# The second block's sequence and context as two instruction streams in turn

## The chip, the core and the metric

The kernel runs on one core of a Trainium2 chip. The number that counts is the time of one execution on the device, in microseconds (us); the runs give a median and a spread, and one further execution was recorded by the hardware profiler. Five engines take part: TensorE (PE, matmuls, with its weight loads PEld), VectorE (DVE), ScalarE (ACT), GpSimd (POOL) and SyncE (SP), which issues the loads. Each engine works through a queue of its own in order and waits for the others by semaphores.

## What is computed

Two transformer blocks in a row, all in float32. The first has one stream of 512 tokens. The second has two: the sequence (512 tokens, `h`) and a context (256 tokens, `hc`), which share all weights. Of the reference, the second block is what matters here:

```python
for i in range(DEPTH_2):                      # 2 layers
    last = i == DEPTH_2 - 1
    h = ffn_half_step(h, g_ffn1[i], m[0], m[1], m[2], w13_ffn1[i], w2_ffn1[i])
    hc = ffn_half_step(hc, g_ffn1[i], mc[0], mc[1], mc[2], w13_ffn1[i], w2_ffn1[i])
    z = n_lat @ w_in[i]
    zc = n_ctx @ (w_in[i][:, OFF_KV:OFF_G] if last else w_in[i])
    # keys and values of both; the sequence attends to both, the context to itself
    y = mix_heads(z, jnp.concatenate([k, kc], axis=1), jnp.concatenate([v, vc], axis=1), rope, *mix_p) @ w_out[i]
    h = h + m[5] * y
    h = ffn_half_step(h, g_ffn2[i], m[6], m[7], m[8], w13_ffn2[i], w2_ffn2[i])
    if not last:
        yc = mix_heads(zc, kc, vc, None, *mix_p) @ w_out[i]
        hc = hc + mc[5] * yc
        hc = ffn_half_step(hc, g_ffn2[i], mc[6], mc[7], mc[8], w13_ffn2[i], w2_ffn2[i])
```

A half step is a norm, `silu(a) * b` of two products 1024 by 2816, and a product back to 1024. `mix_heads` joins a Fourier mixer, attention, a gated mixer and a pooling mixer. So the sequence's attention of a layer needs the context's keys and values of that layer, and those need the context's first half step of that layer; nothing of the context needs the sequence.

## The kernel before

Tokens lie on the free axis and features on the partitions, so a product is 128 output features at a time: 8 tiles of 128 input features, each in three matmuls (`products`, L1753 to L1755), since a float32 operand is split in a high and a low part. A weight block of 128 columns is thus 24 matmuls of 512 columns for the sequence and 24 of 256 for the context.

A block goes through four stages: SP loads it into one of 4 `stage` buffers (`load_block`), ACT copies the high part into one of 3 slots (`split_block`, L1455), DVE (even block numbers, L2129) or POOL (odd ones, L1381) subtracts it for the low part, and PE uses it. `weights` asks for the next split block when it hands out the current one, and that is where the next block's copy stands in ACT's queue.

The code is a walk in Python that every engine makes for itself; each keeps the calls that are its own. The order of the walk is the order of every queue. Small closures are let in at fixed places: `jobs`, and `background`, one piece of the modulation each (a load of 512 KB, 2 + 14 operations of DVE, L2181 and L2184, one small matmul L1775), of which `have_vectors` forces those that are needed.

In the second block `half_step` takes both streams: `swiglu` fetches a block once and multiplies sequence and context with it, in groups of 8, 8 and 6 tiles of the hidden features (`GROUPS`); after a group the products back (`w_down`) are summed into `h`. A background job stands at each tile and at each of the 8 output tiles of a group. Then `mixers` runs for the context and then for the sequence, each alone; in layer 1 the context's stops at keys and values. Before each part stands a norm: squares, a sum by a matmul of ones (L1767), root and reciprocal (`residual_root`), and 8 tiles of `norm_tile` and `norm_low`. The banks 0 to 3 of PSUM are `banks` (products), 4 to 7 `mix` (all else); attention takes all eight in pairs.

## Time and profile before

| | us |
|---|---|
| median of 3 runs | 4099.03 |
| lowest, highest | 4095.73, 4102.06 |
| the profiled execution | 4101.93 |
| its span, first to last instruction | 4100.1 |
| PE busy | 3692.7 (90%) |
| DVE busy | 2276.9 (56%) |
| ACT busy | 1086.1 (26%) |
| POOL busy | 803.9 (20%) |

Of the span, the first block takes the first 1114 us, the rest is the second block. PE is busy in nine tenths of it; the mean clock that it was granted is 0.941 of full speed. In the 40 slices of the page PE's digit falls to 5 to 8 in four places of the second block, where the feed-forward parts end and the norms and mixers stand, and the clock's digit falls with it.

### The profile page before, as it was taken

The numbers are of one execution on the slowest core, as the hardware profiler recorded it, in microseconds if no ns is written. First come the engines' busy times: TensorE is split into PE (matmuls) and PEld (weight loads), VectorE is DVE, ScalarE is ACT, GpSimd is POOL, SyncE is SP. The second block draws the span as 40 slices with busy tenths as digits, with TensorE's granted clock in tenths as the row PEclk, the third lists the DMA queues.
The fourth block names the chain that finished last, engine by engine and source line by source line (L and its number), as shares of the span: only waits on it lengthen the run. The fifth ranks groups of instructions, "written<-read, shape, count | busy, mean of one in ns | idle before, by whom it ended". The sixth has DMA issues, their size and how long they took to land. (4 is left out here: it accounts for less than half of the span.)

```text
span 4100.1 us, 47478 instructions
## 1 busy us (share of the span) xinstructions
PE 3692.7 (90%) x19008; PEld 2977.6 (73%) x19008; DVE 2276.9 (56%) x4939; ACT 1086.1 (26%) x1685; POOL 803.9 (20%) x488
## 2 busy tenths in 40 slices
PE   5888997999889999877889999998999997888997
PEld 3655885788678888755447888887888884457886
DVE  5564556755566666744445666686666534434333
ACT  3354002322321211233243212123212133333222
POOL 1012101222330101223113121232000032012222
PEclk9998787999999999988999999998999997999999
DMA  5532003444323333333102333332333312112332
GB/s 158 149 98 69 1 1 88 113 118 123 88 65 98 105 99 103 94 90 98 42 16 81 85 108 98 108 98 77 93 108 99 92 48 81 32 41 82 93 93 67
DMA packets 663805, 348.35 MB, mean 85 GB/s; under 512 B 29989, under 2 KB 658919, under 8 KB 663328
## 3 DMA queue, kind: packets, MB, share of 16 engines
q1 hardware_dynamic: 662432, 342.69, 29.8%
q8 instruction: 149, 2.44, 0.3%
q10 hardware_dynamic: 1152, 2.62, 0.2%
q14 instruction: 72, 0.59, 0.0%
HBM read 340.55 MB, written 4.72 MB: 84 GB/s over the span
## 5 line engine op out<-in xcount | busy, mean ns | idle before, releaser
L1753 PE MATMUL psum<-hn_high,high 128*128 128x512 f32 (+2 forms) x3360 | 1234.2, 367 | 133.1 <-DVE hn_low L2159 58.4
L1755 PE MATMUL psum<-hn_high,low 128*128 128x512 f32 (+2 forms) x3360 | 1207.2, 359 | 0.0
L1754 PE MATMUL psum<-hn_low,high 128*128 128x512 f32 (+2 forms) x3360 | 1204.1, 358 | 0.0
L1381 POOL TENSOR_TENSOR low<-stage,high 128x1024 fp32r<-128x1024 f32 (+2 forms) x195 | 478.0, 2460 | 2253.3 <-ACT high L1455 2253.3
L1753 PEld LDWEIGHTS psum<-hn_high,high 128*128 128x128 f32 (+1 forms) x3360 | 641.6, 191 | 264.4 <-DVE hn_low L2159 62.7
L2184 DVE SCALAR_TENSOR_TENSOR partial<-stage,cond,partial 128x128 f32<-128x128 f32 x2304 | 819.8, 429 | 0.0
L1755 PEld LDWEIGHTS psum<-hn_high,low 128*128 128x128 f32 (+1 forms) x3360 | 640.3, 191 | 103.7 <-issue 1.8
L1754 PEld LDWEIGHTS psum<-hn_low,high 128*128 128x128 f32 (+1 forms) x3360 | 642.2, 191 | 95.9 <-issue 2.1
L1455 ACT ACTIVATE high<-stage 128x1024 fp32r<-128x1024 f32 (+3 forms) x440 | 438.1, 1016 | 523.3 <-DMA stage<-in_w_ffn 353.8
L1753 PE MATMUL psum<-hidden_high,high 128*128 128x512 f32 (+1 forms) x1408 | 503.8, 358 | 8.8 <-POOL low L1381 8.7
L1755 PE MATMUL psum<-hidden_high,low 128*128 128x512 f32 (+1 forms) x1408 | 496.6, 353 | 0.0
L1754 PE MATMUL psum<-hidden_low,high 128*128 128x512 f32 (+1 forms) x1408 | 494.9, 352 | 0.0
L2129 DVE TENSOR_TENSOR low<-stage,high 128x1024 fp32r<-128x1024 f32 (+2 forms) x245 | 335.2, 1379 | 173.8 <-ACT high L1455 173.6
L2416 DVE TENSOR_TENSOR tmp<-tmp,psum 128x512 f32<-128x512 f32 (+1 forms) x176 | 103.3, 587 | 392.1 <-PE psum L1755 392.0
L1459 ACT ACTIVATE hidden_high<-tmp 128x512 fp32r<-128x512 f32 (+1 forms) x176 | 97.2, 552 | 812.8 <-DVE tmp L2416 812.8
L1753 PEld LDWEIGHTS psum<-hidden_high,high 128*128 128x128 f32 x1408 | 268.2, 190 | 46.8 <-POOL low L1381 11.8
L1754 PEld LDWEIGHTS psum<-hidden_low,high 128*128 128x128 f32 x1408 | 268.1, 190 | 37.2
L1755 PEld LDWEIGHTS psum<-hidden_high,low 128*128 128x128 f32 x1408 | 267.2, 190 | 37.7
L1646 ACT ACTIVATE tmp<-psum 128x512 f32<-128x512 f32 (+1 forms) x176 | 91.3, 519 | 383.2 <-PE psum L1755 383.1
L2134 DVE TENSOR_TENSOR hidden_low<-tmp,hidden_high 128x512 fp32r<-128x512 f32 (+1 forms) x176 | 104.3, 593 | 108.9 <-ACT hidden_high L1459 108.9
L2413 DVE TENSOR_TENSOR tmp<-tmp,psum 128x512 f32<-128x512 f32 (+1 forms) x176 | 102.3, 581 | 102.8 <-ACT tmp L1646 102.7
L1775 PEld LDWEIGHTS psum<-ones,partial 128*128 128x128 f32 x768 | 112.6, 204 | 54.0 <-DVE partial L2184 41.6
(308 smaller groups left out, 3342.7 us busy)
## 6 DMA issues: line engine op xcount, KB each, us to landing
stage<-in_w_ffn SPq DMA_DIRECT2D x240, 512.0 KB, 4.5
stage<-in_w_ada SPq DMA_DIRECT2D x192, 512.0 KB, 4.0
stage<-in_w_in SPq DMA_DIRECT2D x56, 512.0 KB, 5.1
stage<-in_w_out SPq DMA_DIRECT2D x32, 512.0 KB, 4.1
stage<-in_w_ffn SPq DMA_DIRECT2D x32, 384.0 KB, 4.4
stage<-in_w_gate SPq DMA_DIRECT2D x22, 512.0 KB, 4.0
stage<-in_w_up SPq DMA_DIRECT2D x22, 512.0 KB, 5.2
stage<-in_w_down SPq DMA_DIRECT2D x16, 512.0 KB, 4.5
```

Of the source, the lines that this page charges most:

```text
L1381: self.e.tensor_tensor(low, raw, high.bitcast(F32), ALU.subtract).then_inc(*self.mark("split", n))
L1455: self.e.activation(high, raw, ACT.Copy).then_inc(*self.mark("high", n))
L1459: self.e.activation(high, x, ACT.Copy).then_inc(*self.mark("high_half", key))
L1753: self.e.matmul(out, high[:, i], xh, start=first and i == 0, stop=False)
L1754: self.e.matmul(out, high[:, i], xl, start=False, stop=False)
L1755: done = self.e.matmul(out, low[:, i], xh, start=False, stop=last and i == nk - 1)
L1775: done = self.e.matmul(bank.ap[:, at:at + 1], part.ap[:, i, :], self.mem.ones[:, 0:1], start=both or i == 0, stop=both or i == 1)
L2129: self.e.tensor_tensor(low, raw, high.bitcast(F32), ALU.subtract).then_inc(*self.mark("split", n))
L2134: self.e.tensor_tensor(low, x, high.bitcast(F32), ALU.subtract).then_inc(*self.mark(*key))
L2184: self.e.scalar_tensor_tensor(acc, view[:, k, :], by, acc, ALU.mult, ALU.add).then_inc(*inc)
L2413: self.e.tensor_tensor(s, s, ps_a, ALU.mult).then_inc(*self.mark("gated", key))
L2416: self.e.tensor_tensor(s, s, ps_b, ALU.mult).then_inc(*self.mark("gated_up", key))
```

## The change

The second block becomes two generators. `lead_stream` is the sequence, `side_stream` the context. Each step of them ends in a `yield` with a number, the time for which the stream is taken to have nothing to do, on a clock that `cost` advances by the estimated time of PE. `together` takes the steps in turn: the sequence's whenever it is due, the context's when it is not (the other way round while the context is `urgent`, in its layer 0 mixers). The result is one fixed order for each engine.

- `swiglu` and `half_step` take one stream. The context's half steps (three of them) fetch and split all weight blocks for themselves, in groups of 4, 4, 4, 4, 3 and 3 tiles (`GROUPS_SIDE`); their blocks back are 4 tiles by 256 columns (`wide`). The sequence's first half step of layer 0 has groups of 6, 6, 5 and 5 (`GROUPS_BESIDE`), the others keep 8, 8 and 6.
- A background job stands at each tile of the sequence, at every second output tile of it, and at every second tile of the context.
- Memory: one map for the second block (`block_maps`). The context has temporaries of its own (`side_tmp`), sequence and context have two product banks each, the sequence's attention two pairs and two single banks.
- The table of the token Fourier transform and the gated mixer's weights come through the stages.
- In the mixers the sections `v` and `u` alternate by tile, and steps are split where the other stream may come in. The sequence waits for the context's keys and values before its attention, and in layer 0 for all of its mixers.

The counts of matmuls are the same, 9792 of 512 columns and 5280 of 256 in the products. Of the splits of weight blocks of 384 to 1024 columns there are 670 where there were 434: ACT copies 552 blocks of 1024 columns for 388, DVE subtracts 291 for 220, POOL 261 for 168, and small blocks of 384 to 768 columns come to 118 for 46. ACT_TABLE_LOAD stands 52 times for 32.

```diff
+GROUPS_BESIDE = ((0, 6), (6, 6), (12, 5), (17, 5))
+GROUPS_SIDE = ((0, 4), (4, 4), (8, 4), (12, 4), (16, 3), (19, 3))
...
+    def together(self, lead, side):
+
+        ready = {lead: self.now, side: self.now}
+        while ready:
+            streams = [x for x in ((side, lead) if self.side.urgent else (lead, side)) if x in ready]
+            due = [x for x in streams if ready[x] <= self.now]
+            stream = due[0] if due else min(streams, key=ready.get)
+            self.now = max(self.now, ready[stream])
+            gap = next(stream, None)
+            if gap is None:
+                del ready[stream]
+            else:
+                ready[stream] = self.now + gap
...
     def modulated_norm(self, name, part, gain, shift, after):
+
         T = part.T
         self.bring_two()
-        rinv, ready, t = self.residual_root(part, name)
+        yield from self.residual_root(part, name)
+        rinv, ready, t = self.rooted
...
+        yield 4.0 + T / 128
...
+            if k < KT + 1:
+                yield T / 450
...
-    def swiglu(self, name, parts, w_a, a0, w_b, b0, w_down, gate, meanwhile=None):
...
-                order = list(enumerate(parts))
-                for n, part in order if at else order[::-1]:
...
+    def swiglu(self, name, part, groups, hidden, w_a, a0, w_b, b0, w_down, gate, meanwhile=None):
+
+        T = part.T
+        halves = ((0, KT // 2), (KT // 2, KT)) if part is self.main else ((0, KT),)
+        for first, tiles in groups:
+            wide = tiles == 4
             for f in range(tiles):
                 at = first + f
...
+                yield 0
+                n, slot, view = self.weights(w_b, 0, KT, b0 + at * P)
+                if at and (part is self.main or at % 2):
                     self.pump_background()
...
+                self.gate_tile(key, bank_a.ap[:, 0:T], t, s)
+                bank_a.free = [("gated", key)]
+                bank_b = part.banks.next()
...
+                self.up_tile(key, bank_b.ap[:, 0:T], s, hidden[0][:, f, :], hidden[1][:, f, :], part.hidden_free)
+                bank_b.free, t.free = [("gated_up", key)], [("hidden", key)]
+                yield 0
...
+                if self.events and part is self.main and f % 2:
                     self.pump_background()
...
     def second_block(self):
-        main, side = self.main, self.side
-        for layer in range(2):
...
-            self.half_step([main, side], layer, "g_ffn1", 0)
-            self.mixers(side, layer, layer == 1)
-            self.mixers(main, layer, False)
...
+        mem, main, side = self.mem, self.main, self.side
+        main.banks, side.banks = Turn(self.banks.spots[0:2]), Turn(self.banks.spots[2:4])
+        self.events.add("second")
+        self.together(self.lead_stream(), self.side_stream())
+        self.whole(self.plain_norm(main, "final2", False))
...
+    def lead_stream(self):
+
+        main, hidden = self.main, self.mem.hidden
+        yield from self.plain_norm(main, "final", True)
+        for layer in range(2):
+            yield from self.half_step(main, layer, "g_ffn1", 0, *((GROUPS, hidden["whole"]) if layer else
+                                                                  (GROUPS_BESIDE, hidden["beside"])))
+            while layer == 0 and "side mixed" not in self.events:
+                yield 3.0
+            yield from self.mixers(main, layer, False)
+            self.boundary(("mixed", layer))
+            main.hidden_free = [("all", ("mixed", layer), x) for x in COMPUTE]
+            yield from self.half_step(main, layer, "g_ffn2", 6, GROUPS, hidden["whole"])
+
+    def side_stream(self):
+
+        side, hidden = self.side, self.mem.hidden["side"]
+        yield from self.half_step(side, 0, "g_ffn1", 0, GROUPS_SIDE, hidden, normed=True)
+        side.urgent = True
+        yield from self.mixers(side, 0, False)
+        side.urgent = False
+        self.events |= {"side mixed", ("kv", 0)}
+        self.boundary("side mixed")
+        side.hidden_free = [("all", "side mixed", x) for x in COMPUTE]
+        yield from self.half_step(side, 0, "g_ffn2", 6, GROUPS_SIDE, hidden)
+        yield from self.half_step(side, 1, "g_ffn1", 0, GROUPS_SIDE, hidden)
+        while ("attention", (0, "main")) not in self.events:
+            yield 3.0
+        yield from self.mixers(side, 1, True)
+        self.events.add(("kv", 1))
```

PE's new order in the second block, in words: 648 of the context's matmuls within the two norms in front of the sequence's first half step; that half step of the sequence (22 tiles) with two blocks of the context in it; then the rest of the context's first half step (888 matmuls of 256 columns) and all its mixers with nothing beside them; then the sequence's mixers with the context's second half step let in, 24 matmuls at a time, up to the sequence's next norm and the one before layer 1; then the sequence's mixers of layer 1 with the context's third half step let in; 1200 matmuls of that half step and the context's keys and values with nothing beside them; then the sequence's attention and what follows, alone.

Three places show it. First ACT in the feed-forward parts of layer 1. Before, both streams' tiles stand between two pairs of copies:

```order
L1455 ACTIVATE high_5_53<-stage_51 128x1024
L1455 ACTIVATE high_6_54<-stage_51 128x1024
L1646 ACTIVATE tmp_58<-psum 128x512
L1459 ACTIVATE hidden_high_126<-tmp_58 128x512
L1646 ACTIVATE tmp_58<-psum 128x256
L1459 ACTIVATE hidden_high_122<-tmp_58 128x256
```

And now ACT where the context runs alone, the same place in layer 1:

```order
L1615 ACTIVATE high_6_54<-stage_51 128x1024
L1615 ACTIVATE high_4_52<-stage_51 128x1024
L1806 ACTIVATE side_tmp_126<-psum 128x256
L1619 ACTIVATE hidden_high_124<-side_tmp_126 128x256
L1615 ACTIVATE high_5_53<-stage_51 128x1024
```

A pair of copies now stands at every tile of 256 columns; the first of a pair (the block of the `up` product of the same tile) stands behind the tile before's `hidden_high`.

Second ACT in the attention of the sequence in layer 0. Before, exponentials and turned weights alone:

```order
L1721 ACTIVATE scores_175,small_67<-psum,small_67 128x768
L1728 ACTIVATE weights_t_174<-psum 128x6x128
L1721 ACTIVATE scores_175,small_67<-psum,small_67 128x768
L1728 ACTIVATE weights_t_174<-psum 128x6x128
L1721 ACTIVATE scores_175,small_67<-psum,small_67 128x768
```

Now:

```order
L1883 ACTIVATE scores_177,small_67<-psum,small_67 128x768
L1615 ACTIVATE high_5_53<-stage_51 128x1024
L1806 ACT_TABLE_LOAD
L1806 ACTIVATE side_tmp_126<-psum 128x256
L1619 ACTIVATE hidden_high_124<-side_tmp_126 128x256
L1890 ACTIVATE weights_t_175<-psum 128x3x128 x2
L1883 ACT_TABLE_LOAD
L1883 ACTIVATE scores_176,small_67<-psum,small_67 128x768
```

The context's copies, its sigmoid and its `hidden_high` came between the rows, with two table loads around them.

Third DVE at the products back of a half step in layer 0. Before, one job stands at each output tile:

```order
L2181 TENSOR_SCALAR partial_68<-stage_51,cond_65 128x128 x2
L2184 SCALAR_TENSOR_TENSOR partial_68<-stage_51,cond_65,partial_68 128x128 x14
L2189 TENSOR_SCALAR mod_0_15_63<-psum,vec_61 128x2
L2294 SCALAR_TENSOR_TENSOR h_main_49<-psum,small_67,h_main_49 128x512
```

Now, in the group of 5 tiles, one at every second:

```order
L2458 SCALAR_TENSOR_TENSOR h_main_49<-psum,small_67,h_main_49 128x512 x2
L2345 TENSOR_SCALAR partial_68<-stage_51,cond_65 128x128 x2
L2348 SCALAR_TENSOR_TENSOR partial_68<-stage_51,cond_65,partial_68 128x128 x14
L2353 TENSOR_SCALAR mod_0_15_63<-psum,vec_61 128x2
L2293 TENSOR_TENSOR low_8_56<-stage_51,high_5_53 128x640
```

The job moved from every output tile of both streams to every second one of the sequence.

## Rows read from the trace of the kernel before

**Rows 1.** Windows: from:to, length; busy us (instructions) of each engine; clock, DMA share, GB/s.
```profile
1114.00:1148.00 34.00, 10.68 (x55) 7.45 (x53) 23.83 (x19) 9.54 (x15) 15.08 (x10) 0.65 0.11 31
...
1733.00:1855.00 122.00, 82.46 (x460) 65.71 (x460) 56.27 (x119) 47.54 (x103) 28.07 (x27) 0.82 0.29 79
1855.00:1894.00 39.00, 25.33 (x194) 23.94 (x194) 15.20 (x20) 14.30 (x21) 16.26 (x13) 0.89 0.38 113
1894.00:2051.00 157.00, 127.96 (x470) 77.86 (x470) 65.61 (x96) 44.59 (x68) 33.84 (x26) 0.86 0.22 63
2051.00:2125.00 74.00, 60.37 (x208) 29.57 (x208) 34.48 (x72) 32.36 (x55) 0.00 (x0) 0.91 0.00 0
2125.00:2179.00 54.00, 46.87 (x192) 36.98 (x192) 18.96 (x27) 20.86 (x32) 24.20 (x19) 0.97 0.27 79
2179.00:2221.00 42.00, 35.10 (x169) 28.33 (x170) 27.79 (x41) 15.89 (x23) 17.84 (x12) 0.92 0.17 48
...
2778.00:2836.00 58.00, 42.48 (x183) 34.11 (x184) 34.84 (x66) 25.16 (x41) 20.84 (x19) 0.76 0.23 64
...
3366.00:3408.00 42.00, 22.97 (x96) 16.27 (x94) 18.93 (x30) 17.08 (x34) 10.43 (x13) 0.71 0.20 63
3408.00:3567.00 159.00, 128.59 (x470) 78.26 (x470) 66.04 (x97) 44.58 (x68) 33.79 (x26) 0.86 0.21 60
3567.00:3641.00 74.00, 60.38 (x208) 29.59 (x208) 34.43 (x72) 32.82 (x56) 0.00 (x0) 0.91 0.00 1
```

**Rows 2.** PE's matmuls in order of time: start, length (they overlap), line, operands.
```profile
1108.15 0.39 PE L1753 MATMUL psum<-hidden_high,high 128*128 128x512 f32 x1
1108.38 0.39 PE L1754 MATMUL psum<-hidden_low,high 128*128 128x512 f32 x1
...
1141.79 0.28 PE L1753 MATMUL psum<-hn_high,high 128*128 128x256 f32 x1
1141.91 0.28 PE L1754 MATMUL psum<-hn_low,high 128*128 128x256 f32 x1
```

**Rows 3.** The context's w_out alone, 1870 to 1882, in order of time, four engines.
```profile
1870.07 0.48 DVE L2294 SCALAR_TENSOR_TENSOR h_ctx<-psum,mod,h_ctx 128x256 f32<-128x256 f32 x1 [1.11 <-PE psum L1755]
...
1870.59 0.42 ACT L1477 ACTIVATE tmp<-h_ctx 128x256 f32<-128x256 f32 x1 [2.89 <-DVE h_ctx L2294]
1870.91 1.05 ACT L1455 ACTIVATE high<-stage 128x1024 fp32r<-128x1024 f32 x1
...
1872.04 2.36 POOL L1381 TENSOR_TENSOR low<-stage,high 128x1024 fp32r<-128x1024 f32 x1 [0.21 <-ACT high L1455]
...
1874.45 0.38 PE L1753 MATMUL psum<-mixed_high,high 128*128 128x256 f32 x1 [1.70 <-POOL low L1381]
...
1881.87 0.38 PE L1753 MATMUL psum<-mixed_high,high 128*128 128x256 f32 x1 [1.70 <-POOL low L1381]
```

**Rows 4.** DVE's job beside and without POOL's subtractions, feed-forward part of layer 0.
```profile
1415.20 3.75 DVE L2184 SCALAR_TENSOR_TENSOR partial<-stage,cond,partial 128x128 f32<-128x128 f32 x14
...
1429.42 8.07 DVE L2184 SCALAR_TENSOR_TENSOR partial<-stage,cond,partial 128x128 f32<-128x128 f32 x14
...
1429.67 5.04 POOL L1381 TENSOR_TENSOR low<-stage,high 128x1024 fp32r<-128x1024 f32 x2 [29.16 <-ACT high L1455]
```

**Rows 5.** PE's small matmul of a job, products back of the 6-tile group, layer 0.
```profile
1691.50 0.61 PE L1775 MATMUL psum<-ones,partial 128*128 128x1 f32 x4 [1.23 <-DVE partial L2184]
...
1699.70 0.61 PE L1775 MATMUL psum<-ones,partial 128*128 128x1 f32 x4 [1.24 <-DVE partial L2184]
```

**Rows 6.** PE's waits: line, whom it waited for, us in total, times, longest.
```profile
PE psum L2103 <- DVE scores L2527: 11.6, 9, 2.8
...
PE psum L2066 <- DVE w_sgu L2495: 1.6, 1, 1.6
```

**Rows 7.** A table load of ACT, and the operation behind it.
```profile
1886.16 1.28 ACT L1481 ACT_TABLE_LOAD   x1
1887.45 0.63 ACT L1481 ACTIVATE mean_main<-mean_main 128x512 f32<-128x512 f32 x1
```

681 lines of the change are left out of this document (384 added, 297 removed).

## The prediction

> **What bounds the kernel now.** I read the busy times first: PE works in 90% of the span, so a change can bring only what PE leaves unused. Then the windows of the second block, cut where its parts begin. As unused I count the length less PE's busy time, plus the busy time multiplied by what the clock lacks to 1.00 [rows 1]. Window 1894:2051, for instance, gives 157 - 128 = 29 us, and 128 x 0.14 = 18 us from the clock, 47 in all. In the same way: 27 (1114:1148, the norms in front of layer 0), 54 and 17 (the context's mixers), 47, 19, 9 and 10 (the sequence's mixers, attention, w_out, next norm), 26 (norms in front of layer 1), 26, 48 and 19 (the same in layer 1, up to the end of attention). That is 302 us. The feed-forward parts between them leave next to nothing, but for one place in the sum below. Third, the timeline of single matmuls: on the full clock one of 512 columns starts every 0.23 us, one of 256 every 0.12 [rows 2]. Both price PE's work at its columns, so giving the context blocks of its own adds no time to PE. The matmuls are the same ones; the change decides where the unused 302 us go, and whether new ones arise.
>
> **The context alone** is the new cost, and the trace has a place that shows it: its w_out in layer 0, where a block of 24 matmuls is 2.85 us of PE. PE waits 1.70 us at 1874.45 and again at 1881.87, one wait in 7.42 us, that is in two blocks (5.7 us of work) [rows 3]. The chain reads off the same rows. The sum of one output tile ends, DVE adds it at 1870.07, ACT squares at 1870.59, only then ACT's queue comes to the copy of the next block (1870.91, 1.05 us), POOL subtracts at 1872.04 for 2.36, and PE goes on at 1874.45. So 4.4 us pass from the end of a sum to the next but one block, and PE had 2.85 us of work for them. The same stands in a feed-forward tile now: `gated_up` (DVE), `hidden_high` (ACT), then the copy of the tile's `up` block. Where POOL subtracts, I take 1.7 us a tile; where DVE does (1.2 us for 2.4), 0.6.
>
> - Layer 1, 1200 matmuls alone. All `up` blocks fall on POOL by their number. 11 tiles lie within a group: 11 x 1.7 = 19. Five turns between products out and back, where the last `hidden` part is late, at 1.2: 6. In the last group a square stands before each copy, with 1.07 us of PE to hide it: 8 x 1.4 = 11. Sum 36.
> - Layer 0, 888 matmuls alone. 8 tiles at (1.7 + 0.6) / 2 = 9, four turns 4, the last group 11. Seven jobs: a job takes DVE 3.75 us, and 8.07 with two of POOL's subtractions beside it [rows 4]. It stands before the `gated` that frees one of the context's two banks, so that PE waits; 2 us each, 14. Sum 38.
>
> Bounds of the two together: 14 us (nothing but jobs) and 120 (3 us at each of 27 tiles, 3 at each job, both last groups doubled). I take 74, since rows 3 are the same chain on the same shapes.
>
> The Trainium skill bears on these rows. Its page SBUF — State Buffer, section "SBUF: two separate sides", says that VectorE and GpSimd share one pair of ports as an exclusive lock. Rows 4 agree: 8.07 - 3.75 = 4.3 us longer beside 5.04 us of POOL. If the lock held at each of the 93 full blocks that POOL gains, at 2.4 us, it would take DVE 220 us, in a queue that is 56% busy; this speaks against the change, and is the second rival.
>
> **The norms in front of layer 0** (27 us unused). Now 648 matmuls of the context, 78 us of work, lie there, far more than the 34 us. The old waits go. New ones: 7 tiles at 1.15, 3 jobs at 2, two turns, and some 7 us for the root's reciprocals and the tiles of the norm in the same queues: 23. Gain 4, bounds +20 and -20.
>
> **The context's mixers in layer 0.** By the order they do not run inside the sequence's half step. They stand behind it, as alone as before, because the context reaches them too late; the sequence only waits for them. Their 54 + 17 us stay, but for the sequence's norm that was summed there: gain 4.
>
> **The sequence's mixers in layer 0.** 24 matmuls (2.9 us) come in at each step of the chain. Attention leaves 19 us; 11.6 are PE's waits for DVE's normalised scores, 9 of them, the longest 2.8 [rows 6]; each is shorter than one block. I leave 6 for ACT, which gets copies and table loads there: gain 13. w_out and the next norm, 9 + 10, are covered by 336 matmuls that themselves run with stalls: 9 left, gain 9. Waits such as 1.6 for `w_sgu` [rows 6], six of that kind, 6. Of the 18 us of clock I give back 10. The waits in the sections p, u, v stay, since hardly a block stands there. Together 38; bounds 15 and 70.
>
> ACT loads its tables 20 times more, 1.28 us each, 26 us in all, most of it in this attention; a copy, a load and the next operation fit in the 5.5 us that a row of scores now has. The row has the next operation 0.01 us behind the load (1886.16 + 1.28, then 1887.45) [rows 7]. The Trainium skill, page ScalarE: Activation LUTs, section "What ACT_TABLE_LOAD costs", adds a drain of 1.38 us to each load, by which ACT would lose 53 us; this trace does not show the drain.
>
> **Norms in front of layer 1** (26): 276 matmuls, 33 us, cover them but for some 10. Gain 16, bounds 5 and 20.
>
> **The sequence's mixers in layer 1** (26 + 48 + 19): the small waits 6 and of the clock 12 go. Attention stays uncovered and has two pairs and two single banks for four pairs: 3 more. The context's keys and values, now alone behind its half step, cost what they cost in front of the sequence's. Gain 15, bounds 0 and 35.
>
> **The products back of 6 tiles in layer 0.** PE's small matmul comes every 8.20 us (1691.50, 1699.70) and waits 1.24 for DVE [rows 5], where the work is 18 x 0.35 = 6.3 and a little: 1.6 us at each of 8 tiles in two half steps, 26. It goes, since a job stands only at every second one. New: groups of 5 have 6.9 us of PE for a job (4.4 to 8.7), two sums and a subtraction, 8 x 0.8 = 6; two jobs in a row at group ends and two banks for four, 8. Gain 12, bounds 0 and 20. What hides DVE in the sequence's own tiles is 11.1 us of PE; a job of 8.07 with 3 us of other work just fits.
>
> **Sum.** -4 -4 -38 -16 -15 -12 = -89, +74 for the context alone: -15. The profiled execution took 4101.9, so 4087; it lies 2.9 above the median, which gives 4084.
>
> **Rivals.**
> 1. The stalls of the alone stretches are hidden, because the copies run further ahead than in w_out. For it: one of the two copies a tile waits for nothing in ACT's queue. Against: rows 3. Then 24 of the 38, the 36 and 8 of the norms go: 4084 - 68 = 4016.
> 2. It ends slower, through the queues that both streams share. 121 of the context's 228 blocks now stand among the sequence's norms and mixers; each brings 1.05 us to ACT and 1.2 to DVE or 2.4 to POOL, in front of an operation of the sequence's chain. At 0.12 us each (15 / 121) the gain is gone, at 0.6 they cost 73: 4157. For it: the job in rows 4, more than doubled by POOL. Against: DVE is 42% and ACT 28% busy in 1894:2051 [rows 1], and the filled waits give room. The place is the sequence's mixers of layer 0.
> 3. The table loads carry the drain of that page, 20 x 1.38 = 28 us on the path: 4112. Against: rows 7.
>
> **How the numbers follow.** A measurement tells this kernel's time from no change at about 0.2%, 8 us: 4091 and 4107. My forecast has a chance of 0.48; from 4045 to 4125 is its own range, since the gains of 89 and the cost of 74 are each known to some 25; of it 0.27 is faster, 0.12 the same, 0.09 slower. Rival 1 has 0.20 (faster), rival 2 0.28 (slower, but for 0.03 the same), rival 3 0.04 (slower). Faster 0.47, same 0.15, slower 0.38. The range reaches to both rivals and cuts their far ends: 4010 to 4150.
>
> **What would show it.** In the profile after: stretches in which PE runs matmuls of 256 columns alone, some 145 us in layer 0 and 180 in layer 1, where it waits for the subtraction of a block at L1541 (POOL), 1.5 to 2 us a tile. Attention of layer 0 with PE busy over 90% and a clock of 1.00; of layer 1 as before. No cycle of 8.2 us in the products back. My sum is wrong if the alone stretches run at 5.7 us a tile (then rival 1), or if PE in the sequence's mixers of layer 0 still waits 40 us (rival 2).

## The result and the profile after

The changed kernel takes 4387.47 us (median of 4 runs, 4384.61 to 4391.09), the kernel before 4100.55 (4 runs): a ratio of 1.0697, with an interval of 1.0684 to 1.0711. It is slower by 287 us. I had forecast 4084, with a range up to 4150.

The heads of the two pages, first of the changed kernel (span, then busy time, share and instructions of each engine):

```profile
span 4389.2 us, 48940 instructions
PE 3777.8 (86%) x19008; PEld 3046.1 (69%) x19008; DVE 2510.6 (57%) x5128; ACT 1314.4 (30%) x1973; POOL 1059.7 (24%) x615
```

The span is 289 us longer, with the same matmuls. PE's busy time rose by 85 us, for the most part by the clock: its mean is 0.927 where it was 0.941. The rest is PE standing still. The windows of the second block in the changed kernel, cut at the same places of the program as [rows 1] (columns as there):

```profile
1117.00:1260.00 143.00, 98.65 (x665) 94.19 (x666) 93.43 (x151) 55.84 (x75) 54.94 (x31) 0.86 0.39 114
1260.00:1702.50 442.50, 408.00 (x1784) 333.06 (x1784) 323.55 (x769) 100.12 (x130) 90.95 (x44) 0.95 0.45 125
1702.50:1862.00 159.50, 122.20 (x917) 118.15 (x918) 100.83 (x215) 52.72 (x82) 54.91 (x32) 0.93 0.47 137
...
1975.50:2062.50 87.00, 54.43 (x339) 50.92 (x340) 42.51 (x70) 35.09 (x55) 37.27 (x29) 0.76 0.29 85
2062.50:2226.00 163.50, 142.09 (x692) 100.07 (x690) 68.38 (x115) 51.25 (x75) 34.54 (x23) 0.94 0.33 93
2226.00:2397.00 171.00, 139.87 (x807) 106.50 (x806) 99.39 (x204) 76.37 (x122) 31.47 (x13) 0.92 0.30 88
...
2520.00:2937.00 417.00, 390.76 (x1724) 318.53 (x1723) 302.57 (x689) 97.48 (x121) 94.58 (x42) 0.97 0.44 123
2937.00:3010.00 73.00, 48.83 (x282) 45.60 (x282) 36.91 (x80) 26.96 (x43) 24.91 (x19) 0.78 0.39 106
...
3624.00:3826.00 202.00, 161.26 (x1279) 152.53 (x1280) 106.43 (x141) 73.31 (x111) 73.33 (x40) 0.98 0.47 135
```

The first line is the norms in front of layer 0 with 648 of the context's matmuls in them: they hold 78 us of work at full rate and take 143. The third and the last are the stretches of the context alone; those at 1975.50, 2062.50 and 2226.00 are the context's w_out with the norms, the sequence's mixers and its attention.

So that stages of different content can be compared, I take from each stage's length PE's work at full rate: its matmuls, at 0.227 us for 512 columns and 0.117 for 256 in the products, and at the shortest usual distance of their kind elsewhere. What remains is lost, to waits or to the clock. "Before" is the same stage of the kernel before; the last column is what the prediction's sum had.

| stage | lost before | lost after | change | forecast |
|---|---|---|---|---|
| norms in front of layer 0 | 29.5 | 64.9 | +35 | -4 |
| sequence's first half step, layer 0 | 32.3 | 74.4 | +42 | -12 |
| context alone, layer 0 | none | 54.4 | +54 | +38 |
| context's mixers, w_out, norms | 80.2 | 102.4 | +22 | -4 |
| sequence's mixers and attention | 78.1 | 88.1 | +10 | -38 with the next |
| its w_out and next norm | 20.5 | 39.3 | +19 | |
| sequence's second half step, layer 0 | 36.6 | 54.6 | +18 | 0 |
| norms in front of layer 1 | 24.4 | 39.8 | +15 | -16 |
| sequence's first half step, layer 1 | 15.3 | 41.2 | +26 | 0 |
| norms and mixers, layer 1 | 85.0 | 70.5 | -15 | -15 |
| context alone and its keys, layer 1 | none | 66.3 | +66 | +36 |
| attention to the end | 70.9 | 78.1 | +7 | 0 |

The changes sum to 300 where the span grew by 289. Both traces hold the same number of matmuls (19008), so the 11 us are an error of the rows: the cuts between stages and the distance taken for the small matmuls move each change by up to 5 us. Two rows of layer 1 are not like for like: the context's keys and values with their norm lose some 16 us, which before stand in "norms and mixers" and after in "context alone". Counted in one place, the norms, mixers and keys of layer 1 change by +1 and not by -15, and the context alone costs 105.

Three groups then: **alone** +105 where the forecast was +74, the **sequence's own feed-forward parts** +86 where it was -12, and the **fills** (norms, mixers, attention, w_out, keys) +103 where it was -77. Of the 103, 22 are the row of the context's mixers, w_out and norms, most of which runs alone as before. Within the fills the sequence's mixers without attention did gain, 16 us in layer 0 and 20 in layer 1; the attention of layer 0 behind them lost 27. PE's waits in 1117 to 3980 (line, whom it waited for, us, times, longest), before:

```profile
PE psum L1753 <- POOL low L1381: 36.4, 13, 7.1
...
PE psum L1753 <- DVE low L2129: 9.5, 8, 3.6
```

and after:

```profile
PE psum L1915 <- POOL low L1541: 129.6, 61, 6.5
PE psum L1915 <- DVE low L2293: 71.2, 34, 7.5
PE psum L1915 <- DVE side_tmp L2577: 49.2, 17, 7.5
...
PE psum L1915 <- DVE partial L2348: 23.5, 11, 4.5
```

From 1117 to its last matmul PE is idle for 470 us after and 266 before; 155 of these 204 are waits for a block whose low part is late: 201 against 46. The rows of four places show how it comes to that.

**Alone**, layer 1, one tile. The answer to [rows 3]: the chain and the 1.7 us are as forecast.

```profile
3675.90 0.42 DVE L2582 TENSOR_TENSOR side_tmp<-side_tmp,psum 128x256 f32<-128x256 f32 x1 [1.95 <-PE psum L1917]
...
3676.35 0.42 ACT L1619 ACTIVATE hidden_high<-side_tmp 128x256 fp32r<-128x256 f32 x1 [2.86 <-DVE side_tmp L2582]
...
3676.68 1.99 ACT L1615 ACTIVATE high<-stage 128x1024 fp32r<-128x1024 f32 x2
...
3677.80 2.36 POOL L1541 TENSOR_TENSOR low<-stage,high 128x1024 fp32r<-128x1024 f32 x1 [6.25 <-ACT high L1615]
...
3680.30 0.36 PE L1915 MATMUL psum<-hn_high,high 128*128 128x256 f32 x1 [1.79 <-POOL low L1541]
```

**In a norm**, in front of layer 0. The context's copy stands in ACT's queue behind the norm tile's `hn_high`; a job starts on DVE and POOL's subtraction takes 4.33 us beside it. PE waits 5.88. And `hn_high` of the next tile waits 5.19 us for POOL, which is with the context's block: each stream stops the other.

```profile
1210.52 0.63 ACT L1650 ACTIVATE hn_high<-tmp 128x512 fp32r<-128x512 f32 x1
1210.54 3.76 DVE L2348 SCALAR_TENSOR_TENSOR partial<-stage,cond,partial 128x128 f32<-128x128 f32 x14
1211.05 1.04 ACT L1615 ACTIVATE high<-stage 128x1024 fp32r<-128x1024 f32 x1
1212.17 4.33 POOL L1541 TENSOR_TENSOR low<-stage,high 128x1024 fp32r<-128x1024 f32 x1 [8.81 <-ACT high L1615]
...
1216.64 0.55 PE L1915 MATMUL psum<-hn_high,high 128*128 128x256 f32 x1 [5.88 <-POOL low L1541]
...
1217.28 0.63 ACT L1650 ACTIVATE hn_high<-tmp 128x512 fp32r<-128x512 f32 x1 [5.19 <-POOL tmp L1552]
```

**In attention**, layer 0. Attention keeps two pairs of banks, which leaves two single ones in `mix`. A job takes one of them for its small matmul and gives it back with `mod`; PE waits for that bank, 5.79 us, and behind the wait the same matmuls run at 2.77 us for four (1.46 at 2304.14).

```profile
2304.14 1.46 PE L2259 MATMUL psum<-keys,queries 96*128 96x512 f32 x4
...
2308.97 5.84 DVE L2348 SCALAR_TENSOR_TENSOR partial<-stage,cond,partial 128x128 f32<-128x128 f32 x14
...
2314.99 0.90 PE L2267 MATMUL psum<-eye,scores 128*128 128x128 f32 x3 [5.79 <-DVE mod L2353]
...
2315.69 2.77 PE L2259 MATMUL psum<-keys,queries 96*128 96x512 f32 x4
```

**In the sequence's own half step**, where no context block stands. Here a group of 6 tiles ends. SP's queue waits for the stage buffer that a job holds; the job's last operation ends at 1365.05, SP issues the next two blocks at 1365.16, the copy begins at 1369.20, POOL ends at 1372.89, and PE has waited 3.72 us. The profile puts the wait down to the job, since that ended last.

```profile
1365.16 0.99 SPq L466 DMA_DIRECT2D stage<-in_w_ffn  x2
...
1369.20 1.06 ACT L1615 ACTIVATE high<-stage 128x1024 fp32r<-128x1024 f32 x1 [11.16 <-DMA stage<-in_w_ffn]
...
1370.34 2.55 POOL L1541 TENSOR_TENSOR low<-stage,high 128x1024 fp32r<-128x1024 f32 x1 [10.37 <-ACT high L1615]
...
1373.03 0.77 PE L1915 MATMUL psum<-hn_high,high 128*128 128x512 f32 x1 [3.72 <-DVE partial L2348]
```

### The profile page after: what moved, and what is told of

Its sections match the earlier page's. It is cut to its first block and busy times, and to the rows that moved or that the text cites. A ratio compares the mean times of both kernels' runs of the same rounds, so it can differ in the third digit from the quotient of the medians.

```text
span 4389.2 us, 48940 instructions
## 1 busy us (share of the span) xinstructions
PE 3777.8 (86%) x19008; PEld 3046.1 (69%) x19008; DVE 2510.6 (57%) x5128; ACT 1314.4 (30%) x1973; POOL 1059.7 (24%) x615
## 5 line engine op out<-in xcount | busy, mean ns | idle before, releaser
L1915 PE MATMUL psum<-hn_high,high 128*128 128x512 f32 (+3 forms) x3552 | 1329.8, 374 | 299.9 <-POOL low L1541 75.6
L1917 PE MATMUL psum<-hn_high,low 128*128 128x512 f32 (+3 forms) x3552 | 1294.5, 364 | 0.0
L1916 PE MATMUL psum<-hn_low,high 128*128 128x512 f32 (+3 forms) x3552 | 1291.1, 363 | 0.0
L1541 POOL TENSOR_TENSOR low<-stage,high 128x1024 fp32r<-128x1024 f32 (+3 forms) x322 | 742.6, 2313 | 2271.3 <-ACT high L1615 2271.3
L1915 PEld LDWEIGHTS psum<-hn_high,high 128*128 128x128 f32 (+2 forms) x3552 | 698.6, 197 | 460.8 <-issue 121.8
L1615 ACT ACTIVATE high<-stage 128x1024 fp32r<-128x1024 f32 (+4 forms) x676 | 652.0, 980 | 564.4 <-DMA stage<-in_w_ffn 327.6
L1917 PEld LDWEIGHTS psum<-hn_high,low 128*128 128x128 f32 (+2 forms) x3552 | 699.1, 197 | 105.5 <-issue 0.9
L1916 PEld LDWEIGHTS psum<-hn_low,high 128*128 128x128 f32 (+2 forms) x3552 | 700.4, 197 | 97.2 <-issue 1.0
L2293 DVE TENSOR_TENSOR low<-stage,high 128x1024 fp32r<-128x1024 f32 (+4 forms) x354 | 480.0, 1359 | 300.3 <-ACT high L1615 298.8
L1546 POOL TENSOR_TENSOR mean_main<-mean_main,tmp 128x512 f32<-128x512 f32 x63 | 84.3, 1337 | 270.3 <-ACT tmp L1637 270.3
```

The source lines that it names most:

```text
L1541: self.e.tensor_tensor(low, raw, high.bitcast(F32), ALU.subtract).then_inc(*self.mark("split", n))
L1546: self.e.tensor_tensor(total, total, sq, ALU.add).then_inc(*self.mark("squares", name, k))
L1615: self.e.activation(high, raw, ACT.Copy).then_inc(*self.mark("high", n))
L1915: self.e.matmul(out, high[:, i], xh, start=first and i == 0, stop=False)
L1916: self.e.matmul(out, high[:, i], xl, start=False, stop=False)
L1917: done = self.e.matmul(out, low[:, i], xh, start=False, stop=last and i == nk - 1)
```

## The experiments

Four causes were to be told apart: W, the additional blocks by themselves; C, the place of their copies in ACT's queue; J, the jobs; S, the subtractions. "Stage" lengths below are taken between the same matmuls of PE's order in two traces. Where a cut is measured in both kernels, what the change itself is charged with is the difference.

**1. Own blocks in the old order (`b_own`).** Part of the change alone: the context fetches and splits its own blocks, nothing else moves.

```diff
-                n_a, slot_a, wa = self.weights(w_a, 0, KT, a0 + at * P)
-                n_b, slot_b, wb = self.weights(w_b, 0, KT, b0 + at * P)
...
-                for n, part in order if at else order[::-1]:
+                for turn, (n, part) in enumerate(order if at else order[::-1]):
+                    n_a, slot_a, wa = self.weights(w_a, 0, KT, a0 + at * P)
+                    n_b, slot_b, wb = self.weights(w_b, 0, KT, b0 + at * P)
...
-                n_d, slot, view = self.weights(w_down, first * P, tiles, f * P)
...
                 for n, part in enumerate(parts):
+                    n_d, slot, view = self.weights(w_down, first * P, tiles, f * P)
```

> The kernel before, in its own order, but with the context loading and splitting every weight block of its feed-forward parts for itself instead of sharing the sequence's: about 200 more blocks of load, copy and subtraction, nothing moved. Theory W (the 287 us are the work of the additional blocks: SP's loads, ACT's copies, the subtractions of DVE and POOL): 4300 to 4400. Theory Q (it is where they stand: behind operations of the other stream and with too little of PE's work beside them): here each context tile of 5.7 us lies between sequence tiles of 11.1 us, so most is hidden: 4110 to 4180.

Measured: 4374.29, ratio 1.0662 (1.0641 to 1.0684), +272. Nearly the whole loss of the change, with no stretch alone and no fill in it. The three shared half steps grew from 558, 557 and 529 us to 642, 627 and 611, 236 of the 272. A context tile there:

```profile
1302.25 0.69 DVE L2416 TENSOR_TENSOR tmp<-tmp,psum 128x512 f32<-128x512 f32 x1 [2.44 <-PE psum L1755]
...
1302.97 0.63 ACT L1459 ACTIVATE hidden_high<-tmp 128x512 fp32r<-128x512 f32 x1 [5.69 <-DVE tmp L2416]
...
1303.51 1.99 ACT L1455 ACTIVATE high<-stage 128x1024 fp32r<-128x1024 f32 x2
...
1304.63 2.35 POOL L1381 TENSOR_TENSOR low<-stage,high 128x1024 fp32r<-128x1024 f32 x1 [14.90 <-ACT high L1455]
...
1307.04 0.39 PE L1753 MATMUL psum<-hn_high,high 128*128 128x256 f32 x1 [2.07 <-POOL low L1381]
```

The sequence's tile of 11.1 us in front of it hides nothing, since the copy stands behind that tile's `hidden_high` and starts only when the tile's last sum is done. The cover was there in time, but not in the order of the queue. Theory Q (4110 to 4180) fell; W stands by its number, though the rows already show that the copy's place belongs to it.

**2. Copies two blocks ahead, everywhere (`a_ahead`).**

```diff
         self.bring_to(target)
+        if self.second and split and len(later) > 1:
+            while self.brought <= later[1]:
+                unsplit = not plan[self.brought][5]
+                if all(x.taken for x in self.stages.spots) or not unsplit and all(x.taken for x in self.slots.spots):
+                    break
+                self.bring_to(self.brought)
```

> The changed kernel, but in the second block the copy of a block is asked for two blocks ahead instead of one, wherever a slot is not in use; in the context's tiles both copies then stand in front of the sigmoid and not behind hidden_high. Theory C (most of what was lost is the copy that stands behind a dependent operation in ACT's queue): the 1.7 us at each tile alone go and a part of the waits for low in the norms and mixers: 4388 - 34 - 20 - 40 = about 4290. If the jobs (theory J) or the load and work of the blocks (theory W) are what costs, it stays within 25 us of 4388.

Measured: 4418.16, ratio 1.077 (1.0752 to 1.0788), 31 us slower than the changed kernel. Neither theory. By stages two things are mixed: the context alone in layer 1 fell from 203 to 177 us, its w_out and norms from 87 to 73, and the sequence's three half steps grew by 42, 38 and 31. There PE now waits for the product with the sigmoid, which frees one of a stream's two banks: both copies stand ahead of the sigmoid, and wait in ACT's queue for a slot or for their load. PE's waits over the whole span:

```profile
PE psum L1923 <- DVE side_tmp L2585: 107.4, 23, 9.4
PE psum L1923 <- DVE tmp L2585: 88.7, 45, 7.2
```

and ACT's in the sequence's first half step (1257 to 1742), for a slot that PE frees:

```profile
ACT high L1623 <- PE psum L1925: 58.5, 19, 11.9
```

In the same stage of the changed kernel (1260 to 1702) ACT waits 8.2 us in 4 times for such a slot, and 108 us for loads where it is 184 here.

**3. The same, behind the sigmoid (`a_late`), and there for the context's tiles only (`a_late_side`).** `ahead` brings the next two split blocks if a slot and a stage are free. In `a_late` it stands at three places; in `a_late_side` those in `swiglu` have `if part is self.side` ahead of them.

```diff
                 bank_a.free = [("gated", key)]
+                self.ahead()
                 bank_b = part.banks.next()
...
                     slot.free = [("down_sum", key)]
+                    self.ahead()
...
                 slot.free = [done]
+                self.ahead()
                 if k + nk == n_k:
```

> The changed kernel with the copies two blocks ahead, but placed behind the sigmoid of a tile (and behind the products of a block of w_in, w_out and w_down, in front of what depends on them). The run with the copies ahead of the sigmoid lost 42, 38 and 31 us in the sequence's three shared-queue feed-forward parts and gained 26 alone in layer 1, 14 in w_out and the next norms, 11, 9 and 6 in mixers. Theory C (the copy behind a dependent operation costs PE a wait, and the loss of that run was only the late sigmoid with two banks): the gains stay and the losses go: 4388 - 80 = about 4310. If the gains came from elsewhere, 4370 or more.

> The changed kernel with the copies two ahead behind the sigmoid as in the run that gave 4326, but in the feed-forward parts only for the context's tiles. In that run the sequence's own feed-forward parts lost 16, 16 and 8 us. If it was the third copy, which there waits for PE's block in front of the tile's hidden_high: they come back, 4326 - 40 = 4286. If it was another parity of the blocks (which of them fall to POOL) or the jobs: about 4326.

Measured: `a_late` 4325.99, ratio 1.0553 (1.0538 to 1.0569); `a_late_side` 4278.79, ratio 1.0428 (1.0411 to 1.0446). 61 and 109 us of the changed kernel's 287 come back by moving copies, at the same work. Theory C holds. In `a_late_side` the stages are shorter: alone in layer 1 203 to 177 us, norms in front of layer 0 143 to 131, context's w_out and norms 87 to 78, norms in front of layer 1 73 to 63. The sequence's half steps of layer 0 are 439 and 412 us in `a_late_side`, 459 and 433 in `a_late`: what they had lost was the third copy in their own tiles.

**4. The fills taken away (`a_nofill`).**

```diff
-                ready[stream] = self.now + gap
+                ready[stream] = self.now + (gap if gap == 3.0 or stream is side else 0.0)
```

> The changed kernel, the same two streams, but the sequence is taken as always due: the context comes in only where the sequence waits for its keys, values or squares. Some 2500 of the context's 256-column matmuls then no longer stand among the sequence's norms and mixers but alone. My prediction's account of the fills (they fill waits that stay otherwise, about 85 us, and alone the blocks run at 0.155 us a matmul instead of 0.1175): 4388 + 85 + 95 = 4570. If the fills bring nothing (the stages with fills lose 87 us more than the same stages before, as the two traces show): 4388 - 87 + 95 + some 15 of clock = about 4410.

Measured: 4402.49, ratio 1.0733 (1.0712 to 1.0755), 15 us slower. Some 2500 matmuls of the context, 300 us of PE's work, stand in PE's gaps in the changed kernel and alone in this one, and that is worth 15 us. My account of the fills wanted 180. In both places such blocks make PE wait: standing in the gaps saves 15 us against standing alone.

**5. The jobs cut to 4 of 16 operations in both kernels (`a_jobs`, `b_jobs`).** Three quarters of the modulation's sum are left out.

```diff
-        for k in range(KT):
+        tiles = 2 if both and self.second else KT
+        for k in range(tiles):
```

> The changed kernel with the background jobs of the second block cut to 4 of their 16 operations of DVE (two of eight input tiles are summed; the loads, the small matmul and the places stay). It leaves out three quarters of that sum. Theory J (a job in DVE's queue stands in front of the operation for which PE waits): 121 jobs, about 2.8 us of DVE less each; if a third of that is on PE's path, 4388 - 110 = 4280 or less, and the same cut gives the kernel before far less. Theories C and W: about the same gain as the cut gives the kernel before, 25 to 40 us: 4355.

> The kernel before with the same cut of its jobs (4 of 16 operations, three quarters of that sum left out). The 8.20 us cycle of the products back of the 6-tile groups falls to PE's 6.6: 26 us, and a few us elsewhere: 4100 - 30 = 4070 by every theory; it is the measure that the cut in the changed kernel is held against.

Measured: 4234.64 (ratio 1.0322, 1.0301 to 1.0343) and 4064.32 (0.9907, 0.9887 to 0.9927): 153 us against 38. 115 of the 287 need a whole job. Of the 153, 101 lie in the sequence's own half steps: 443, 416 and 407 us fall to 394, 381 and 390, by which theory J holds there.

**6. The subtractions cut to 128 of 1024 columns in the second block: in the changed kernel (`a_low`), on POOL alone (`a_low_pool`), in the kernel before (`b_low`), and with own blocks (`b_own_low`).** The low parts are stale but for one input tile in eight.

```diff
             self.wait_ge("high", n)
+            if self.second:
+                low, raw, high = low[:, 0:P], raw[:, 0:P], high[:, 0:P]
```

> The changed kernel with every subtraction for the low part in the second block cut to its first 128 columns (the low parts are then stale but for one input tile in eight; loads, copies, places and all waits stay). PE's waits for low sum to 210 us in the changed kernel and to some 60 before. Theory S (the subtraction's 2.4 us on POOL and 1.2 on DVE are the link that makes the chain too long, and POOL also lengthens the jobs): 4388 - 140 or more, 4250 or less. Theory C alone (the copy's place): each wait shortens by at most the subtraction's time, and others take its place: 4300 to 4340.

> The kernel before with the subtractions of the second block cut to 128 columns (low parts stale but for one input tile in eight), the measure for the same cut in the changed kernel, which gave 214 us. PE's waits for low there are some 66 us in all, 54 of them in the second block, and the jobs of rows 4 lose their company on POOL. 4103 - 50 = about 4053 by every theory; under 4010 if the subtractions cost the kernel before as much as the changed one, which would take the 214 us out of the explanation.

> The kernel before with own blocks for the context (4374) and the same cut of the subtractions. Theory S (the time between a copy and the end of its subtraction, at 24 matmuls of 2.85 us a block): the 272 us fall to 100 or less, 4374 - 50 - 150 = 4175. If the place of the copy alone made the 1 to 2 us at each context tile, the wait shortens by 1.2 to 2.3 us a block as well and the two can't be told apart by this run; if it is the load or the DMA, it stays over 4300.

> The changed kernel with only POOL's subtractions of the second block cut to 128 columns; DVE's stay whole. The cut of both gave 214 us. If POOL's 2.3 us (and the lengthening of DVE's operations beside it) carry it: 4388 - 150 = 4240 or less. If DVE's queue carries it: 4388 - 90 = 4300 or more.

| | us | ratio (interval) |
|---|---|---|
| a_low | 4174.06 | 1.0172 (1.0152 to 1.0193) |
| b_low | 4040.28 | 0.9849 (0.9829 to 0.9868) |
| b_own_low | 4119.47 | 1.0041 (1.0025 to 1.0057) |
| a_low_pool | 4245.85 | 1.035 (1.0329 to 1.0371) |

The cut takes 213 us from the changed kernel and 62 from the one before: 151 of the 287 hang on the subtractions' time. Own blocks cost 272 with whole subtractions and 4119 - 4040 = 79 with short ones. So most of what I called W is not load, copy or DMA but the subtractions, and of these POOL's part is the larger: 142 of the 213. The runs do not separate two ways in which they cost. They lengthen the chain from copy to low; and they lengthen the jobs, whose operations take 444 ns on average in the changed kernel, 378 in `a_low` and 377 in `a_low_pool`. The waits in 1117 to 3980 of own blocks, first with whole, then with short subtractions:

```profile
PE psum L1753 <- POOL low L1381: 199.3, 76, 15.8
PE psum L1753 <- DVE low L2129: 72.3, 52, 14.3
```

```profile
PE psum L1757 <- POOL low L1385: 75.6, 50, 13.7
PE psum L1757 <- DVE low L2135: 29.1, 27, 12.4
```

**7. Two causes at once.** `a_late_jobs` has the edits of `a_late` and `a_jobs`; `b_own_ahead` those of `b_own` and `a_ahead`.

> The changed kernel with both edits: copies two ahead behind the sigmoid (61 us) and the jobs cut to 4 of 16 operations (153 us; three quarters of their sum left out). If the two causes are apart: 4388 - 214 = 4174. If they are one cause (a block is late because DVE is with a job, whoever is ahead), the second gains less: 4200 to 4235. If the copies ahead lost their 16, 16 and 8 us in the sequence's feed-forward parts to jobs: 4388 - 214 - 40 = 4134.

> The kernel before with the context's own blocks (4374 without more) and the copies two blocks ahead as in the run that gave 4053. Of the 272 us that the own blocks cost, 236 lie in the three shared feed-forward parts, where PE waits for low at nearly every context tile. Theory C (the copy of a block stands in ACT's queue behind a dependent operation): most of it goes, 4374 - 49 - 140 = about 4185. If the waits are the time of the load, copy and subtraction themselves: 4374 - 49 = 4325.

Measured: `a_late_jobs` 4115.67, ratio 1.003 (1.0019 to 1.0041), where 4174 would be the sum of the two gains; the third figure, 4134, was nearest. The copies ahead and the jobs hinder each other: together the two edits give 272 us, one by one 61 and 153. `b_own_ahead` took 4460.0, ratio 1.0869 (1.0847 to 1.0891), 86 us more than without, where theory C wanted 190 less. Here copies wait for a slot only twice, 2.5 us, in the first shared half step (1200 to 1870). What waits there is DVE: the subtraction of a block that was asked for ahead stands in DVE's queue, in front of the job, until its copy is done, 125 us where it was 35 in `b_own`. PE's small matmul waits for the job behind it. PE over the whole span, then DVE in that half step:

```profile
PE psum L1783 <- DVE partial L2192: 162.1, 63, 5.4
```

```profile
DVE low L2137 <- ACT high L1463: 124.6, 55, 7.2
```

(In `b_own` the first of these waits was 34 us over the whole span.) This run tells nothing for or against the copy's place; it shows that "earlier" in a queue is earlier than somebody.

**8. Subtractions on DVE alone (`a_dve`), nothing left out.**

```diff
-        if n % 2:
+        if n % 2 and not self.second:
...
-        if n % 2 == 0:
+        if n % 2 == 0 or self.second:
```

> The changed kernel with every subtraction of the second block on DVE (1.2 us a block of 1024 columns when POOL is quiet) instead of every other one on POOL (2.3 us); nothing is left out. Cutting POOL's alone gave 142 us. If a block's latency and the lengthening of DVE's operations beside POOL are what costs, most of that stays: 4388 - 100 = about 4290. If DVE's queue (57% busy, with about 250 subtractions, 300 us more) is as tight as the jobs' run suggests, the gain is lost again: 4370 to 4420.

Measured: 4350.27, ratio 1.0606 (1.0587 to 1.0625), 37 us less than the changed kernel, between the two figures. 285 subtractions more on DVE raised its busy time by only 34 us. The two groups of the page that say why (count, then busy us and mean ns), in the changed kernel:

```profile
L2348 DVE SCALAR_TENSOR_TENSOR partial<-stage,cond,partial 128x128 f32<-128x128 f32 x2304 | 853.1, 444 | 0.0
L2293 DVE TENSOR_TENSOR low<-stage,high 128x1024 fp32r<-128x1024 f32 (+4 forms) x354 | 480.0, 1359 | 300.3 <-ACT high L1615 298.8
```

and in `a_dve`:

```profile
L2350 DVE SCALAR_TENSOR_TENSOR partial<-stage,cond,partial 128x128 f32<-128x128 f32 x2304 | 681.4, 370 | 0.0
L2295 DVE TENSOR_TENSOR low<-stage,high 128x1024 fp32r<-128x1024 f32 (+4 forms) x639 | 739.4, 1171 | 436.9 <-ACT high L1617 434.4
```

The 259 us of new subtractions are paid for by 172 us that the jobs get shorter, and by others. The Trainium skill, page SBUF — State Buffer, section "SBUF: two separate sides", says that VectorE and GpSimd share a pair of ports by an exclusive lock. These lines agree with it: what POOL subtracts was mostly taken out of DVE's time already.

**9. What gained in the kernel before.** `b_ahead` is the edit of `a_ahead` there; `b_place` puts a job only at every second output tile of the 6-tile groups; `b_best` is both, `b_best_dve` adds the edit of `a_dve`.

```diff
-                if len(parts) > 1:
+                if len(parts) > 1 and (tiles == 8 or f % 2):
                     self.pump_background()
```

> The kernel before with the copies of the second block asked for two blocks ahead wherever a slot is free. The 1.7 us waits of the context's w_out (rows 3) and of like places in the mixers' sections go: theory C gives 4100 - 15 = 4085; in the feed-forward parts one more copy stands ahead of the sigmoid, with four banks and 16.8 us of PE beside it: nothing. Should the late sigmoid matter here too: 4100 to 4130.

> The kernel before, but with a background job only at every second output tile of the 6-tile groups (the jobs that fall away there run later, at other tiles or where they are forced). The cut of the jobs' work gave 38 us. If that came from the 8.20 us cycle of those products (rows 5), moving them gives 12 to 25 us: about 4083; if it came from jobs at forced places, this makes it longer: 4100 to 4120.

> The kernel before with the two edits that gained: copies two ahead (49 us) and a job only at every second output tile of the 6-tile groups (20 us). They lie in different stages (mixers and w_out; products back), so 4102 - 69 = 4033; if the moved jobs then fall into the places that the first edit filled, 4045.

> The kernel before with copies two ahead and fewer jobs in the 6-tile groups (4037), and every subtraction of the second block on DVE; nothing is left out. A job then takes 3.75 us everywhere and not 8.07, and POOL's 2.4 us go from the sections of the mixers and w_out: 4037 - 15 = about 4022. If DVE becomes late in the products back: 4037 to 4050.

| | us | ratio (interval) |
|---|---|---|
| b_ahead | 4053.36 | 0.9885 (0.9868 to 0.9901) |
| b_place | 4082.24 | 0.9953 (0.9938 to 0.9968) |
| b_best | 4037.04 | 0.9836 (0.982 to 0.9852) |
| b_best_dve | 4030.40 | 0.9825 (0.9809 to 0.984) |

The two gains add up as expected, and `b_best_dve` is faster than both kernels of this case, by 71 and 357 us, and leaves nothing out. The copies ahead gave 49 where I expected 15. By stages: the sequence's mixers 157 and 159 us to 145 and 144, the context's 120 to 107, its w_out 40 to 33. In the first shared half step, with four banks and both products ahead of the sigmoid, the edit changes nothing (558 to 557). The last 6.6 us, between `b_best` and `b_best_dve`, are less than half of what I expected, and the intervals overlap.

## Why the prediction was wrong

**The unused time** before was read rightly, and so was PE's price by columns. The wrong steps are in what was set against it.

**The context alone: the mechanism right, the size too small.** 1.7 us a tile where POOL subtracts was forecast, 1.79 measured in the row above. As waits the sum was good: PE is idle for 41 us in layer 1 and 37 in layer 0, 78 where I had 74. The 105 that were lost, within the bound of 120, hold 27 more, which I had left out: the time by which PE's busy time exceeds its work at full rate, 17 of it in layer 0, on a clock of 0.93. Within the 37 of layer 0 the parts were wrong. The seven jobs weigh more than the 14 that I gave them, since PE waits for the product behind them (1702 to 1862):

```profile
PE psum L1915 <- DVE side_tmp L2577: 19.5, 7, 5.3
```

The edit that cuts the jobs takes this stage from 159 us to 143. The low parts cost 9 us where I had 20.

**The fills: the sign wrong.** The sentence "The old waits go. New ones ..." priced new waits for tiles, jobs and turns, and took 77 us of gain. What I did not price is that a context block among dependent operations of the sequence is in the same queues of ACT, DVE, POOL and SP, so that it comes late itself and delays them: 103 us lost instead, 180 us off. Over the 121 blocks of my rival 2 that is 1.5 us a block, where I had taken 0.6 as its far case. The rival had a price less than half, and its place, the sequence's mixers of layer 0, was right only for their attention. I had it with PE busy over 90% on a clock of 1.00 and a gain of 13 us; it was busy for 82% (139.87 of 171.00) on 0.92 and lost 27. The mixers' other sections gained 16, and the norms lost 35 and 15, which I had not named. The sign that I gave for this rival, 40 us of PE's waits there, did come: PE is idle for 21 us in the mixers and 31 in attention. The run without fills shows the net: 15 us for 300 us of work that was moved.

**The sequence's own half steps: the step "What hides DVE in the sequence's own tiles is 11.1 us of PE; a job of 8.07 with 3 us of other work just fits" was wrong.** I took 12 us as gained and the other two parts as untouched; they lost 86. Inside a group it fits: but for the first tiles behind a turn PE there runs without a wait. It fails in a group's products back and at the turn to the next group, of which `GROUPS_BESIDE` makes four where there were three. In the products back of the two groups of 5 six waits sum to 20 us, where I had put 6. At the turn a job holds a stage buffer that SP's queue waits for, and before, the context's matmuls had covered the last `hidden` part and the next blocks; that they were the cover is read from the two traces, no run tried it. PE's idle time in the three parts rose from 21 us to 77, which is 56 of the 86; the rest is the clock behind the waits. I had counted the context's share of PE as work to be moved and never as the cover that it was. The cut jobs give 101 us back there, and the stage without fills is as long (434 us for the same 1584 matmuls and its jobs), so it isn't the fills.

**The clock** fell instead of rising. I had counted 10 and 12 us of it as gained in the mixers. In the windows of both mixers it is 0.94, up from 0.86, so that this part was right. It was lost again in the sequence's half steps (0.95 to 0.98, from 0.99 and 1.00) and in two stretches of the context (0.93 alone in layer 0; 0.76 in its w_out, from 0.89), where PE had waited. Alone in layer 1 it is 0.98.

**Rival 1** (no stalls alone) was refuted by the rows. **Rival 3** too: a table load is followed at once by the next operation in the changed kernel's attention as well.

```profile
2308.78 1.28 ACT L1806 ACT_TABLE_LOAD   x1
...
2310.07 0.39 ACT L1806 ACTIVATE side_tmp<-psum 128x256 f32<-128x256 f32 x1
```

The Trainium skill, page ScalarE: Activation LUTs, section "What ACT_TABLE_LOAD costs", gives the load the length that these rows show; the drain that it adds to it is not in them, nor behind any of 29 of the 52 loads, where the next operation begins 0.01 us later (in the other 23 it waits for its operand). The measurement decides.

**The range** ended at 4150 because every bound was a bound of waits at the places I had named, each from a row of before. The kernel before had blocks with only 2.85 us of PE to them in few places, the context's mixers and w_out, and I took their price for a price of those places. The one experiment that would have told, own blocks in the old order, costs 272 us by itself.

What stays open: the cuts of jobs (115), of subtractions (151) and the copies' place (60, as 109 against 49, by edits that are not the same) exceed the 287 together, so they are links of one chain and can't be given shares. How much of the jobs' 115 us is DVE's time, how much the stage buffer and how much the bank in attention was not tried apart.

## What to carry to other kernels

Before work is moved into another stream's gaps, count what it brings to each in-order queue, not to the engine that has the gap: here 300 us of matmuls in PE's gaps were worth 15 us. Two streams that share a loaded block hide its load, copy and subtraction; a block of its own needs as much PE time as its chain is long (here some 4.5 us from the sum it stands behind, against 2.85), and if it doesn't have that, it must be prepared further ahead. An operation that prepares the next block belongs in front of the dependent operations of the current one, but behind those that free what PE waits for next.

## What the hardware showed that I had not expected

Moving 158 subtractions from POOL to DVE in the kernel before (`b_best` to `b_best_dve`) raised DVE's busy time from 2263.3 to 2270.4 us, 7 us for 158 operations of 1.2. The page lines of the jobs there, first with POOL at work, then without:

```profile
L2192 DVE SCALAR_TENSOR_TENSOR partial<-stage,cond,partial 128x128 f32<-128x128 f32 x2304 | 818.5, 429 | 0.0
```

```profile
L2192 DVE SCALAR_TENSOR_TENSOR partial<-stage,cond,partial 128x128 f32<-128x128 f32 x2304 | 673.7, 368 | 0.0
```

The jobs alone get 145 us shorter. In this kernel, to have every other subtraction on POOL saved DVE next to nothing.
